# Second half of the experts' down product as three fp32r products, with the rests of the weights formed by Pool

## What is computed

```python
N_EXPERTS, TOP_K, D_EXPERT, D_MODEL = 64, 8, 256, 1024

def swiglu(h, w_gu, w_down):
    gate, up = jnp.split(h @ w_gu, 2, axis=-1)
    return (jax.nn.silu(gate) * up) @ w_down

def expert_block(acc, blk):
    tok, wts, e = blk
    out = swiglu(h_pad[tok], w_gu[e], w_down[e])
    return acc.at[tok].add(out * wts[:, None]), None
```

## Time and profile before

| | us |
|---|---|
| median of 3 runs | 2160.59 (2159.59 to 2163.52) |
| span of the profiled execution | 2159.3 |
| PE busy in it | 2064.3 (96%) |
| DVE busy | 1225.8 (57%) |
| ACT busy | 964.7 (45%) |
| Pool busy | 243.5 (11%) |

### The profile page before, as it was taken

One profiled execution on the slowest core, in us unless ns is written; L12 is line 12 of the kernel. 1 busy time (PEld: TensorE's weight loads), 2 busy tenths in 40 slices (PEclk: granted clock), 3 DMA queues, 4 the chain that ended last, 5 costly groups with the idle time before them and its releaser, 6 DMA issues.

```text
span 2159.3 us, 32847 instructions
## 1 busy us (share of the span) xinstructions
PE 2064.3 (96%) x12130; PEld 1676.7 (78%) x12131; DVE 1225.8 (57%) x2038; ACT 964.7 (45%) x1349; POOL 243.5 (11%) x217
## 2 busy tenths in 40 slices
PE   7998979999999899999989999999999999999998
PEld 3787977889766566777666666998988898899898
DVE  3858578446766547667756656456652344423433
ACT  4337375233366456666656654335332224312322
POOL 0004023000222222222223220000000000000000
PEclk9999999999999999999999999999999999999999
DMA  9831111263689779999989974211122223222221
GB/s 354 288 114 44 56 59 60 81 258 125 268 309 333 251 231 348 339 359 362 364 282 343 370 254 175 95 62 57 59 79 89 87 79 111 95 98 97 82 95 59
DMA packets 76667, 392.52 MB, mean 182 GB/s; under 512 B 16321, under 2 KB 32833, under 8 KB 46049
## 3 DMA queue, kind: packets, MB, share of 16 engines
q1 hardware_dynamic: 57506, 357.33, 44.5%
q0 software_dynamic: 19008, 33.22, 6.2%
HBM read 384.03 MB, written 42.48 MB: 198 GB/s over the span
## 4 chain that ended last, share of the span: by engine, by line
PE 66%; DVE 4%; ACT 2%; issue 2%; DMA 2%; SPq 0%; DVEq 0%; POOLq 0%; ACTq 0%
PE bank L3330 16%; PE bank L2269 9%; PE bank L2247 5%; PE bank L2251 5%; PE bank L2250 5%; PE bank L3013 3%; PE bank L3014 3%; PE bank L3015 3%; PE bank L2999 2%; PE bank L2998 2%; PE bank L3000 2%; PE bank L2235 2%; PE bank L2203 1%; DMA ffn_sums<-moe_work 1%; DVE moe_gu_rest L2028 1%
## 5 line engine op out<-in xcount | busy, mean ns | idle before, releaser
L2615 DVE TENSOR_TENSOR b_w_rest<-ring,b_w_high 128x2048 fp32r<-128x2048 f32 x63 | 144.4, 2292 | 182.0 <-ACT b_w_high L2610 181.6
L2269 PE MATMUL bank<-moe_work 128*128 128x512 f32 x512 | 237.5, 605 | 0.0
L2247 PE MATMUL bank<-moe_gu_high,moe_x_high 128*128 128x512 f32 x512 | 208.6, 407 | 15.4 <-issue 9.0
L2028 DVE TENSOR_TENSOR moe_gu_rest<-moe_work,moe_gu_high 128x2048 fp32r<-128x2048 f32 x64 | 143.8, 2289 | 114.3 <-ACT moe_gu_high L1773 114.2
L2028 DVE TENSOR_TENSOR moe_gu_rest<-ring,moe_gu_high 128x2048 fp32r<-128x2048 f32 x64 | 143.8, 2289 | 105.9 <-ACT moe_gu_high L1773 105.9
L2251 PE MATMUL bank<-moe_gu_high,moe_x_rest 128*128 128x512 f32 x512 | 202.5, 395 | 0.0
L2250 PE MATMUL bank<-moe_gu_rest,moe_x_high 128*128 128x512 f32 x512 | 202.0, 395 | 0.0
L2610 ACT ACTIVATE b_w_high<-ring 128x2048 fp32r<-128x2048 f32 x63 | 120.5, 1912 | 176.7 <-PE bank L3330 126.8
L3014 PE MATMUL bank<-b_w_rest,b_h_high 128*128 128x256 f32 x608 | 173.1, 285 | 0.0
L2269 PEld LDWEIGHTS bank<-moe_work 128*128 128x128 f32 x512 | 92.4, 191 | 89.9 <-issue 89.5
L3013 PE MATMUL bank<-b_w_high,b_h_high 128*128 128x256 f32 x544 | 157.3, 289 | 2.2 <-DVE b_h_rest L2645 1.1
(11 more groups left out here) (509 smaller groups left out, 4968.0 us busy)
## 6 DMA issues: line engine op xcount, KB each, us to landing
ring<-in_stream_dram SPq DMA_DIRECT2D x105, 1024.0 KB, 4.9
moe_work<-in_experts_dram SPq DMA_DIRECT2D x32, 2048.0 KB, 12.2
moe_work<-in_experts_dram SPq DMA_DIRECT2D x64, 1024.0 KB, 7.2
ring<-in_experts_dram SPq DMA_DIRECT2D x32, 2048.0 KB, 13.7
X<-in_stream_dram SPq DMA_DIRECT2D x16, 512.0 KB, 7.8
mixer_work<-in_stream_dram SPq DMA_DIRECT2D x16, 512.0 KB, 6.5
X<-in_x_dram SPq DMA_DIRECT2D x8, 512.0 KB, 8.7
ffn_sums<-mixer_work SPq DMA_DIRECT2D x8, 512.0 KB, 5.5
```

Of the source, the lines that this page charges most:

```text
L2028: v.tensor_tensor(WL[o % 4][h], guslot[o % 4][:, HALF * h:HALF * (h + 1)], WH[o % 2][h], ALU.subtract).then_inc(s["w_rest"], 1)
L2247: first = mm(banks[2][:, :], xh[:, k, :], wh[h][:, c], start=(k == 0), stop=False)
L2269: product = mm(banks[bank + j][:, :], HDT[o % 2][:, k, :], w[:, k, 512 * j:512 * (j + 1)], start=(k == 0), stop=(k == 1))
L2615: nc.vector.tensor_tensor(WL[u % FEED], raw(u), high_at(u), ALU.subtract).then_inc(s["w_rest"], 1)
```

## The change

1. `down` for k = 1 is three fp32r products instead of one fp32 product; k = 0 stays fp32. Further blocks do the same.
2. The rounded down weights DH (second half, 128x1024) are written by ACT in a new step `dn_high(u)`; their rests DL by Pool in a new step `dn_rest(u)`, in place in the slot.
3. The hidden values' second half is split too: ACT's `copy_hdt` becomes two copies of 128 columns, and DVE has a new step `hdt_rest` at the end of its body.
4. DVE's `w_rest` is cut in two: the first half stays at the head of the body, the second comes behind `x_rest`.
5. `onehot` is one instruction of 512 elements instead of four of 128.
6. One DH slot takes the place of the last tile of X. So SP writes that tile to DRAM ahead of the loop and reads it back behind the last-but-one down product; ACT's first `dn_high`, DVE's routing and DVE's `mixed(3)` wait for these.

```diff
+            sp.dma_start(dram["last_rows"][:, :], X[:, NT - 1, :]).then_inc(s["rows_moved"], 16)
             sp.dma_start(unit(LOADU[1]), stream[LOADU[1]]).then_inc(s_unit[1], 16)
...
             sp.wait_ge(s["dn_done"], NE - 1)
+            sp.wait_ge(s["rows_moved"], 32)
+            sp.dma_start(X[:, NT - 1, :], dram["last_rows"][:, :]).then_inc(s["rows_moved"], 16)
             unit_in(0)
...
+            def dn_rest(i, o):
+                after(pool, "down_highs", i, o, 1, 3)
+                nc.gpsimd.tensor_tensor(DL[o % 2], dnslot[o % 2][:, D:2 * D], DH[o % 2], ALU.subtract).then_inc(
+                    s["down_rest"], 1)
...
                 if exists(i, u + 3):
                     gather(i, u + 3)
+                dn_rest(i, u)
                 looped_blocks(pool, i, u, done, find_further, further)
...
+            def dn_high(i, o):
+                act.wait_ge(s_dn[o % 2], 16 * (o // 2 + 1) + 32 * i)
+                after(act, "dn_done", i, o - 2, 1)
+                if isinstance(i, int) and 4 * i + o == 0:
+                    act.wait_ge(s["rows_moved"], 32)
+                nc.scalar.activation(DH[o % 2], dnslot[o % 2][:, D:2 * D], ACT.Copy).then_inc(s["down_highs"], 1)
...
                     x_high(i, u + 1)
+                dn_high(i, u)
                 woven_block(act, i, u, done, first_further, later_further, ordinary)
...
                 if exists(i, u + 1):
-                    w_rest(i, u + 1)
+                    w_rest(i, u + 1, 0)
                 hidden(i, u)
                 if exists(i, u - 1):
                     place(i, u - 1)
                 if exists(i, u + 1):
                     x_rest(i, u + 1)
+                    w_rest(i, u + 1, 1)
...
                 more_blocks(dve, i, u, done, find_further, further)
+                hdt_rest(i, u)
...
             def down_ready(i, o, bank=4):
-                after(pe, "hdt_ready", i, o, 1)
+                after(pe, "down_highs", i, o, 3, 3)
+                after(pe, "hidden_rest", i, o, 1)
+                after(pe, "down_rest", i, o, 1)
...
+            def down_products(bank, j, k, o, plain, high, rest):
+
+                c = slice(512 * j, 512 * (j + 1))
+                if k == 0:
+                    return mm(bank[:, :], plain, dnslot[o % 2][:, c], start=True, stop=False)
+                mm(bank[:, :], high, DH[o % 2][:, c], start=False, stop=False)
+                mm(bank[:, :], high, DL[o % 2][:, c], start=False, stop=False)
+                return mm(bank[:, :], rest, DH[o % 2][:, c], start=False, stop=True)
```

More of the change, by code:

```diff
@@ L1502, in moe @@
     HIDX = EXR[:, 516:772]
-    SGX, HDTX = EXR[:, 0:256], grid(EXR[:, 256:512], 2)
+    SGX, HDTX = EXR[:, 0:256], EXR[:, 256:384]
+    HDTXH, HDTXL = (exact(f"hidden_further_{n}", AT_ADAROW + o, P) for n, o in (("high", 384), ("rest", 776)))
     IDXX, WCX = [EXR[:, 512 + k:513 + k].bitcast(I32) for k in range(2)], [EXR[:, 514 + k:515 + k] for k in range(2)]
@@ L1997, in onehot @@
                 after(dve, "idx_done", i, o - 2, 1)
-                for t in range(NT):
-                    last = v.tensor_scalar(ONEHOT[o % 2][:, t, :], DEALT, PM[:, t, index(i, o)], None, ALU.is_equal)
-                last.then_inc(s["onehot"], 1)
+                v.tensor_tensor(ONEHOT[o % 2], DEALT.rearrange("p (a q) -> p a q", a=1).to_broadcast([P, NT, P]),
+                                PM[:, :, index(i, o)].to_broadcast([P, NT, P]), ALU.is_equal).then_inc(s["onehot"], 1)
             def indices(i, o):
@@ L2022, in place, with w_rest, hdt_rest @@
                     s["placed"], 1)
-            def w_rest(i, o):
-                for h in range(2):
-                    after(dve, "w_high", i, o, 1 + h, 2)
-                    v.tensor_tensor(WL[o % 4][h], guslot[o % 4][:, HALF * h:HALF * (h + 1)], WH[o % 2][h],
-                                    ALU.subtract).then_inc(s["w_rest"], 1)
+            def w_rest(i, o, h):
+                after(dve, "w_high", i, o, 1 + h, 2)
+                v.tensor_tensor(WL[o % 4][h], guslot[o % 4][:, HALF * h:HALF * (h + 1)], WH[o % 2][h],
+                                ALU.subtract).then_inc(s["w_rest"], 1)
+            def hdt_rest(i, o):
+                after(dve, "down_highs", i, o, 3, 3)
+                v.tensor_tensor(HDTL[o % 2], banks[3][:, P:2 * P], HDTH[o % 2], ALU.subtract).then_inc(s["hidden_rest"], 1)
             def x_rest(i, o):
@@ L2101, in _ @@
             shared_hidden(0)
-            w_rest(0, 0)
+            w_rest(0, 0, 0)
+            w_rest(0, 0, 1)
             shared_hidden(1)
@@ L2177, in _ @@
             weighted(3)
+            dve.wait_ge(s["rows_moved"], 48)
             mixed(3)
@@ L2320, in further_down @@
             def further_down(i, u, n):
-                pe.wait_ge(s["x_he"], n + 1)
+                pe.wait_ge(s["x_he"], 2 * n + 2)
+                pe.wait_ge(s["x_hid"], 2 * n + 2)
+                after(pe, "down_rest", i, u, 1)
                 pe.wait_ge(s_dn[u % 2], 16 * (u // 2 + 1) + 32 * i)
-                w = dnslot[u % 2].rearrange("p (k c) -> p k c", k=2)
                 for j in range(2):
                     for k in range(2):
-                        last = mm(banks[6 + j][:, :], HDTX[:, k, :], w[:, k, 512 * j:512 * (j + 1)],
-                                  start=(k == 0), stop=(k == 1))
+                        last = down_products(banks[6 + j], j, k, u, HDTX, HDTXH, HDTXL)
                     last.then_inc(s["x_dn"], 1)
```

40 lines of the change are left out of this document (25 added, 15 removed).

## The result

The changed kernel takes **2206.82 us** (median of 4 runs, 2203.19 to 2209.1) where the kernel before, run beside it, takes 2162.06: a ratio of 1.0206, 95% interval 1.0181 to 1.023. The sign was forecast, the size was not: 2206.8 lies 33 us above the forecast and 17 above the range. The profiled execution has a span of 2207.4 us, 48.1 more than before.

What follows compares the result with a forecast made beforehand. PE was taken to bound the loop, busy 256.64 of 256.64 us. From 2159.3, products -22.8, stalls +32.4 and edges +4.1 gave 2173.0; with the runs' median 1.3 above the span, 2174 us, range 2146 to 2190.

Steps and rivals of the forecast that it cites:

- Subtraction: Pool's subtraction forming the down weights' rests, not hidden: 2.40 us each.
- Products: PE's down product: passes of 0.43, fp32r products of 0.23, no switch cost; 0.34 us less per block, 22.8 in all.
- Lock: Pool's subtraction and DVE's w_rest, both with SBUF inputs: one waits for the other's whole instruction.
- Stalls: PE ahead of the down product waits 1.7 us for Pool in one of three blocks; 18 x 1.8 = 32.4 us more.
- What hides: dn_high (0.93 us) on ACT, hidden rest, onehot and w_rest's second half on DVE fit in idle time, costing nothing.
- Tail: Behind the last expert: Pool's last subtraction 1.6 us and the parked tile's read-back 1.3 us, 2.9 more.
- a further block's hidden copy and rest are in series, about 0.4 each, three times: 1.2: Edge term at the three further blocks: 1.2 us more, part of the 4.1 us of edges.
- the gather loses: Rival: Pool's gather regularly waits behind w_rest, stalls of 2.8 us, 2192 us; harder stalls (2181 to 2200) had chance 0.18.
- Held by the transfers: Rival: faster, but DMA rate limits heavy stretches of the loop, late down weights hitting dn_high first; 2151 us, chance 0.14.
- No stall: Rival: Pool and DVE run side by side or the subtraction starts early enough, PE never waits; 2142 us, chance 0.12.

Runs made afterwards that it cites:

- before, find behind: Kernel before with w_rest in two halves, indices ahead of the second, and PE's find of further tokens behind gate-and-up: 2139.85 us (ratio 0.9913).
- the run with the list first: Changed kernel with indices (the token list) ahead of w_rest's second half, subtraction still on Pool: 2167.14 us (ratio 1.0029).

## Why the prediction was wrong

Right were the terms that a row stood behind. *Subtraction:* 2.40 us forecast, 2.35 where nothing disturbs it. *Products:* pitches of 0.43 and 0.23, no dearer switch; a regular block without stall takes 9.85 to 10.00, 9.93 forecast. *Lock:* Pool and DVE wait for each other's whole instruction. *Stalls:* 1.62 where 1.7 was worked out, with two or three regular blocks of 9.9 to 10.3 between two of them, mostly. *What hides:* onehot, dn_high (1.06 us, not 0.93), the hidden rest and w_rest's second half cost a regular block nothing. *Tail:* 3.0 against 2.9, though the table shows that 3 us there prove little.

The regular blocks (0 to 11, 18 to 44, 50 to 62: 52 blocks) were to change by 32.4 - 52 x 0.34 = 14.7 and changed by 0.6 + 2.5 + 4.5 = 7.6. The table splits that: without the subtraction they take 524.1 us, 19.1 less than before (17.7 forecast), with it on Pool 550.7, so the stalls and what goes with them cost 26.6 there, not 32.4. They came less often than every third block: of PE's 16 waits for Pool, 12 with 15.6 us in sum lie in these 52 blocks, three (7.4) in the eleven blocks of the next paragraph. The walk-through started from one phase and let it repeat with period three; it repeats with four, and in some stretches longer.

**The step that failed is the term "a further block's hidden copy and rest are in series, about 0.4 each, three times: 1.2".** With the products' gain, the eleven blocks around the further ones were to fall by 14 x 0.34 - 1.2 = 3.6. They rose by 37.7. The miss of 41 there, less 7 in the regular blocks, is the whole error of 34 (2207.4 against 2173.0). The prediction looked at what a further block adds, not at what stands in DVE's queue ahead of the things that PE waits for *there*. In a regular block PE needs the list nowhere, and 2.3 us more ahead of it are hidden. At the head of blocks 13, 14 and 46 PE waits for a one-hot that is last in that queue, and in further_turn it waits for the list itself. Both waits could be read in the trace of before (3.8 and 6.3 us), and both had no cover: what is put ahead of them counts. Without the subtraction they stand at 12.4 and 11.9 us, 2.9 and 1.9 more at each of the three places, with 2.3 us of w_rest's second half newly right ahead (and 0.28 of the hidden rest, for the one-hot). What the runs show of the 41:

- Pool's subtraction: with it gone, these blocks fall by 14.6 (119.5 to 109.7 and 83.5 to 78.7). The rest of the 40 us that it costs lies in the regular blocks, where the prediction had priced it. The one-hot beside it takes 3.66, not 0.95.
- The order on DVE: with the list ahead of w_rest's second half, the waits for the list are 5.3 and not 12.6; with the wait at the head gone, blocks 12 to 17 and 45 to 49 fall by 17.6 and 6.6.
- The clock, which no term had. A mean of 0.89 over 119.5 us and of 0.90 over 83.5 means 13.1 and 8.4 us lost, if PE had worked throughout; before it was 3.9 and nothing. That is up to 17.6 of the 41, and it isn't a cause of its own: it follows PE's longer idle stretches and goes with them, in blocks 12 to 17 of "before, find behind" wholly:

```profile
693.28:783.22 89.94, 83.92 (x372) 57.17 (x370) 49.60 (x99) 46.66 (x60) 27.50 (x17) 1.00 0.72 247
```

These overlap, so they aren't to be added.

Of the rivals, "the gather loses" was right for single blocks (17, 49 and 53 take 14.3, 14.3 and 16.0 us, with stalls of 2.9, 2.9 and 3.0 where 2.8 was worked out; by its own terms, 15.9 + 0.99 + 2.40, that would be 2.7) and wrong as a rule. "Held by the transfers" didn't hold for the changed kernel, whose stalls kept the share at 0.96, but it does hold, in a mild form and just by way of dn_high as was said there, once the stalls are gone: 366 GB/s at a share of 1.00. "No stall" was to be decided by 0.6 us of Pool's time. The run with the list first shows it: the subtraction 2.3 us earlier, and no stall in 27 blocks. The prediction priced the regular blocks of the order that it was given, and nearly rightly; it didn't see that one line moved would have undone 40 us.

The Trainium skill (SBUF — State Buffer, Who interferes with whom) counts tensor_scalar among the operations of DVE that take the shared pair in their two-port modes. The further one-hot is one, with a single full-size input, and it waited for Pool's whole subtraction: the trace agrees (3.66 against 0.95 us). The prediction cited that section for two-input subtractions only.

## What to carry to other kernels

Before putting work on an engine, list every place where the bottleneck engine waits for that engine, rare paths too, and price the work there in full: the eleven blocks around three rare ones grew by 37.7 us, the 52 regular ones by 7.6. When an engine's exclusion seems to cost much, try first to move ahead of it the results that others wait for; here one line's place was worth as much as the whole subtraction. A wait of the matrix engine is dearer than its length where the granted clock falls behind it, and taking out such a wait gained more (20.5 us, of which some 6 may be chance) than the arithmetic that the change was made for (3.7 to 8.0).

## What the runs showed of the hardware

- PE behind an idle stretch: behind 7.15 and 1.01 us of waits close together its records are 0.63 us where 0.40 is usual (granted clock 0.61 over the next 4.1 us); behind 1.62 us in a regular block they aren't (1.00 from 966.9 to 972).
- An indirect transfer issued while DVE forms w_rest takes longer: the gather 2.2 us and not 1.06, the scatter 2.53 us on average and not 1.67, with the subtraction on DVE and so without any on Pool. No wait of PE names either there.
- Reads with indirect transfers among them reach 366 GB/s at a DMA share of 1.00 over 27 blocks, and 376 over single stretches.
- Gaps of PE without a named releaser, 1.5 to 16.0 us in sum in the loop and just behind it, change with every version of the program. They stay unexplained, and no comparison of under some 5 us between two profiles here should be trusted without timed runs.
